# Normed residual steps of an eight-stage transformer kernel, in token halves: the end of each down product, the norm's sum from rounded parts, and the first three up blocks

## The reference, cut to what matters

```python
def rms_norm(x, g):
    xf = x.astype(jnp.float32)
    y = xf * lax.rsqrt(jnp.mean(xf * xf, axis=-1, keepdims=True) + EPS)
    return (y * g.astype(jnp.float32)).astype(x.dtype)

# first block, for each of 2 layers
hn = rms_norm(x, norm_mix_pre[layer])
m = mixer(hn, ...)                      # ends in ... @ w_out
x = x + rms_norm(m, norm_mix_post[layer])
hn = rms_norm(x, norm_ffn_pre[layer])
f = conv_geglu_ffn(hn, ...)             # ends in ... @ w_down
x = x + rms_norm(f, norm_ffn_post[layer])
```

## Time and profile before

| | |
|---|---|
| median of three executions | 2587.75 us |
| the profiled execution, first to last instruction | 2586.1 us |
| TensorE busy | 2557.9 us, 99% |
| VectorE busy | 1661.4 us, 64% |
| ScalarE busy | 1273.8 us, 49% |
| GpSimd busy | 360.5 us, 14% |
| granted TensorE clock, mean | 0.999 of full |

### The profile page before, as it was taken

One profiled execution on the slowest core, in us unless ns is written; L12 is line 12 of the kernel. 1 busy time (PEld: TensorE's weight loads), 2 busy tenths in 40 slices (PEclk: granted clock), 3 DMA queues, 4 the chain that ended last, 5 costly groups with the idle time before them and its releaser, 6 DMA issues.

```text
span 2586.1 us, 35264 instructions
## 1 busy us (share of the span) xinstructions
PE 2557.9 (99%) x12636; PEld 2031.6 (79%) x12636; DVE 1661.4 (64%) x2384; ACT 1273.8 (49%) x2129; POOL 360.5 (14%) x270
## 2 busy tenths in 40 slices
PE   9999999999999999999999999999999999999999
PEld 7855788888787557788888775789988777899887
DVE  4476677643988895677653777587633546687533
ACT  4326544333546895444333577567533425567432
POOL 0020100000103781100000130000610002000800
PEclk9999999999999999999999999999999999999999
DMA  5330222222233442222222230132232221232222
GB/s 215 107 93 25 96 98 97 97 98 95 82 135 118 135 131 73 85 98 94 97 98 97 95 103 1 60 120 99 88 107 96 92 104 50 98 123 99 82 97 97
DMA packets 74689, 250.44 MB, mean 97 GB/s; under 512 B 8748, under 2 KB 8876, under 8 KB 74192
## 3 DMA queue, kind: packets, MB, share of 16 engines
q1 hardware_dynamic: 73488, 240.63, 27.1%
q0 software_dynamic: 944, 8.33, 0.9%
q10 hardware_dynamic: 144, 0.00, 0.0%
HBM read 242.50 MB, written 2.24 MB: 95 GB/s over the span
## 4 chain that ended last, share of the span: by engine, by line
PE 90%; DVE 4%; ACT 2%; issue 1%; POOL 1%; SPq 0%; DMA 0%; DVEq 0%; ACTq 0%; POOLq 0%
PE bank L409 25%; PE bank L410 24%; PE bank L411 24%; PE bank L2199 2%; PE bank L1302 2%; PE bank L1304 2%; PE bank L1303 2%; POOL xT L852 1%; DVE mT L477 1%; PE bank L2751 1%; PE bank L3097 1%; PE bank L1647 1%; PE bank L1636 1%; PE bank L2206 1%; ACT arena L2826 0%
## 5 line engine op out<-in xcount | busy, mean ns | idle before, releaser
L383 DVE TENSOR_TENSOR wlo<-wraw,whi 128x1024 fp32r<-128x1024 f32 x349 | 447.7, 1284 | 444.6 <-ACT whi L360 444.0
L360 ACT ACTIVATE whi<-wraw 128x1024 fp32r<-128x1024 f32 x357 | 375.9, 1055 | 497.6 <-DMA wraw<-in_w 497.5
L409 PE MATMUL bank<-hnhi,whi 128*128 128x512 f32 (+1 forms) x1528 | 596.3, 390 | 0.8 <-DVE wlo L383 0.5
L410 PE MATMUL bank<-hnlo,whi 128*128 128x512 f32 (+1 forms) x1528 | 584.5, 382 | 0.0
L411 PE MATMUL bank<-hnhi,wlo 128*128 128x512 f32 x1392 | 542.1, 389 | 0.0
L409 PE MATMUL bank<-ahi,whi 128*128 128x512 f32 x1184 | 463.5, 391 | 1.8 <-DVE stats L2860 0.6
L410 PE MATMUL bank<-alo,whi 128*128 128x512 f32 x1184 | 460.8, 389 | 0.0
L411 PE MATMUL bank<-ahi,wlo 128*128 128x512 f32 x1184 | 460.8, 389 | 0.0
L409 PEld LDWEIGHTS bank<-hnhi,whi 128*128 128x128 f32 x1528 | 287.3, 188 | 85.1 <-issue 29.2
L410 PEld LDWEIGHTS bank<-hnlo,whi 128*128 128x128 f32 x1528 | 287.4, 188 | 57.8 <-issue 3.4
L411 PEld LDWEIGHTS bank<-hnhi,wlo 128*128 128x128 f32 x1392 | 261.3, 188 | 55.2
(11 more groups left out here) (356 smaller groups left out, 3918.8 us busy)
## 6 DMA issues: line engine op xcount, KB each, us to landing
wraw<-in_w SPq DMA_DIRECT2D x410, 512.0 KB, 3.3
arena<-cs_scratch SPq DMA_DIRECT2D x20, 512.0 KB, 6.0
over_a<-cs_scratch SPq DMA_DIRECT2D x12, 512.0 KB, 6.6
arena<-in_rpb POOLq DMA_DIRECT2D x1, 2880.0 KB, 14.0
out_dram<-xT SPq DMA_DIRECT2D x8, 256.0 KB, 2.0
arena<-in_t_step POOLq DMA_DIRECT2D x2, 897.0 KB, 4.7
mT<-arena SPq DMA_DIRECT2D x28, 64.0 KB, 2.0
arena<-in_t_ab POOLq DMA_DIRECT2D x1, 1472.0 KB, 6.6
```

The costliest lines, as they stand in the source:

```text
L360: act.activation(whi[:, slot * BLOCK:(slot + 1) * BLOCK], wraw[:, slot * BLOCK:(slot + 1) * BLOCK], ACT.Copy).then_inc(sem("w_hi"), 1)
L383: dve.tensor_tensor(low_home(i), wraw[:, slot * BLOCK:(slot + 1) * BLOCK], whi[:, slot * BLOCK:(slot + 1) * BLOCK], ALU.subtract).then_inc ...
L409: pe.matmul(out, wh, ah, start=start, stop=False)
L410: pe.matmul(out, wh, al, start=False, stop=False)
```

## The change

For `d` of 0 to 3, everything from the last two down tiles to the third up block is done in two halves of 256 tokens, A (tokens 0 to 255) and B.

- TensorE multiplies tile K-2 in full into banks 0 to 3 and for A alone into banks 4 to 7, then tile K-1 for A into all banks, then tile K-2 for B into banks 4 to 7, then tile K-1 for B.
- The squares of a half are all added by VectorE (seven additions for each half), the sum is split into a high part (ScalarE) and a low part (VectorE), and TensorE sums over the partitions in two fp32r matmuls of 256 columns, with ones rounded to fp32r, in place of three float32 ones. The five matmuls of `pe_busy` are gone.
- Rows of A are worked through (unit, x, high, low), then rows of B. VectorE updates x for rows 0, 1 and 4 of each half, GpSimd for the other five.
- Up blocks 0 to 2 take A for all eight rows, then B, with block 2 four rows behind.
- The next norm's partition sum stands at row 4 of block 3, before it was at row 1.

The core of the diff:

```diff
+        def pe_up_halves(pe, b0, norm):
...
+            for i, c in enumerate(HALVES):
+                for s in range(KT + LAG):
+                    if s < KT:
+                        pe.wait_ge(sem("norm_hi"), ROWS_BEFORE[norm] + 8 * i + s + 1)
...
+                    k = s - 1
+                    if 0 <= k < KT:
+                        pe.wait_ge(sem("hn_ready"), ROWS_BEFORE[norm] + 8 * i + k + 1)
...
+                    k = s - LAG
+                    if k >= 0:
...
+                        if i == 0 and k == SUM_AT_ROW:
+                            pe_post_sum(pe, d, 1)
...
+        def pe_down_halves(pe, name, K, d):
...
+            ready(K - 2)
+            for m in range(KT):
+                if m < 4:
+                    pe_product(pe, name, At(K - 2), m)
+                else:
+                    half(K - 2, m, 0)
+            ready(K - 1)
+            for m in range(KT):
+                half(K - 1, m, 0, True).then_inc(sem("down_done"), 1)
+            for m in range(4, KT):
+                pe.wait_ge(sem("post_sq"), squared(d, 0, m))
+                mm = half(K - 2, m, HALF)
+            mm.then_inc(sem("w_used"), 1)
+            for m in range(KT):
+                if m == 0:
+                    pe.wait_ge(sem("post_added"), added(d, "scaled"))
+                if m == 3:
+                    pe_post_sum(pe, d, 0)
+                half(K - 1, m, HALF, True).then_inc(sem("down_done" if m < KT - 1 else "w_used"), 1)
...
-            for m in range(KT):
-                wait_down(act, name, K, d, m)
-                act.activation(post_sq(m), bank[m][:, :], ACT.Square).then_inc(sem("post_sq"), 1)
-            act_split(act, At(FIRST[name] + K + 2))
...
+            act_split(act, At(nxt + 1))
+            act.activation(round_ones(), ones, ACT.Copy)
             for m in range(KT):
...
+                square(0, m)
+            square(1, 0)
+            raw(0)
+            sum_high(0)
+            square(1, 1)
+            raw(1)
+            square(1, 2)
+            raw(2)
+            root(0)
+            for m in range(3, KT):
+                square(1, m)
+                if m == 5:
+                    high(0, 0)
+                if m == 6:
+                    high(0, 1)
+            act_split(act, At(nxt + 2))
+            for m in range(2, KT):
+                high(0, m)
+            sum_high(1)
+            root(1)
+            for m in range(KT):
+                high(1, m)
+                act_square(act, m)
...
+            def rows(i, lag, after):
+                for m in range(KT + lag):
+                    if m < KT:
+                        unit(i, m)
+                        if m in X_BY_DVE:
+                            x_add(i, m)
+                    if m >= lag:
+                        low(i, m - lag)
+                    after(m)
+
+            def between(m):
+                if m == 3:
+                    dve_split(dve, At(FIRST[name] + K + 2))
+                if m >= 7:
+                    add(1, m - 4)
+
+            dve_split(dve, At(FIRST[name] + K + 1))
+            dve.wait_ge(sem("post_sq"), squared(d, 0, 0))
+            dve.tensor_scalar(mt(0)[:, 0:HALF], bank[0][:, 0:HALF], col(g, g0), None, ALU.mult).then_inc(sem("post_added"), 1)
+            for m in range(1, KT):
+                add(0, m)
+            sum_low(0)
+            add(1, 1)
+            add(1, 2)
+            rows(0, 2, between)
+            add(1, 6)
+            add(1, 7)
+            sum_low(1)
+            rows(1, 2, lambda m: None)
```

More of the change, by code:

```diff
@@ L576, in pe_up @@
                         mm = three(pe, bank[m.base % 4][:, :], w_parts(i, k * P), hn_parts(k), k == 0, k == KT - 1)
-                        if m.r is None and m.base == first and k == (1 if norm in POSTED else 3):
+                        if m.r is None and m.base == first and k == (4 if norm in POSTED else 3):
                             pe_norm_sum(pe, norm)
@@ L721, in pe_down @@
                     mm.then_inc(sem("w_used"), 1)
-            skew = K - 1 - last
-            for s in range(KT + 2 * skew):
-                if s in (0, 2 * skew):
+            if d < 4:
+                pe_down_halves(pe, name, K, d)
+                return
+            for s in range(KT + 2):
+                if s in (0, 2):
                     k = last + (s > 0)
@@ L727, in pe_down @@
                     pe.wait_ge(sem("w_lo"), b0 + k + 1 + extra(b0))
-                if skew and s < KT:
+                if s < KT:
                     mm = part(At(K - 2), s)
@@ L806, in pe_busy @@
[L806 to L819 removed]
+        SUM_BANKS = (0, 3)
@@ new lines, in wait_half, with squared @@
+        def wait_half(eng, name, K, d, i, m):
+            if i and m == KT - 1:
+                eng.wait_ge(sem("w_used"), FIRST[name] + K + extra(FIRST[name]))
+            else:
+                eng.wait_ge(sem("down_done"), 15 * d + 8 * i + m + 1)
+        SQUARES = ([(0, m) for m in range(KT)] + [(1, 0), ("raw", 0), (0, "sum"), (1, 1), ("raw", 1), (1, 2), ("raw", 2)]
+                   + [(1, m) for m in range(3, KT)] + [(1, "sum")])
+        def squared(d, i, m):
+            return len(SQUARES) * d + SQUARES.index((i, m)) + 1
@@ new lines, in build, with added, post_gain, square @@
+        ADDED = {"scaled": 1, ("sum", 0): 2, ("low", 0): 3, ("sum", 1): 4, ("low", 1): 5}
+        def added(d, what):
+            return len(ADDED) * d + ADDED[what]
+        def post_gain(d, m):
+            return POST[d][0], POST[d][1] + m
+        def act_post(act, name, K, d):
+            g, g0 = NORM_G[d + 1]
+            nxt = FIRST[name] + K
+            def square(i, m):
+                c = HALVES[i]
+                wait_half(act, name, K, d, i, m)
+                act.activation(post_sq(m, c), bank[m][:, c:c + HALF], ACT.Square).then_inc(sem("post_sq"), 1)
+            def raw(m):
+                act.activation(mt(m)[:, HALF:SEQ], bank[m][:, HALF:SEQ], ACT.Copy, scale=col(*post_gain(d, m)))\
+                    .then_inc(sem("post_sq"), 1)
+            def sum_high(i):
+                act.wait_ge(sem("post_added"), added(d, ("sum", i)))
+                act.activation(post_parts(HALVES[i])[0], post_sq(0, HALVES[i]), ACT.Copy).then_inc(sem("post_sq"), 1)
+            def root(i):
+                act.wait_ge(sem("post_sum"), 2 * d + i + 1)
+                act_rsqrt(act, post_sum(i), rstd[:, HALVES[i]:HALVES[i] + HALF], 1.0 / DM, EPS, "post_rstd")
+            def high(i, m):
+                c = HALVES[i]
+                act.wait_ge(*x_added(d, i, m))
+                act.activation(hn_parts(m)[0][:, c:c + HALF], xt(m)[:, c:c + HALF], ACT.Copy, scale=col(g, g0 + m))\
+                    .then_inc(sem("norm_hi"), 1)
+            act_split(act, At(nxt + 1))
+            act.activation(round_ones(), ones, ACT.Copy)
+            for m in range(KT):
+                square(0, m)
[21 more added lines that the diff above has]
+                act_square(act, m)
@@ new lines, in pe_post_sum @@
+        def pe_post_sum(pe, d, i):
+            pe.wait_ge(sem("post_added"), added(d, ("low", i)))
+            if i:
+                pe.wait_ge(sem("post_unit"), 16 * d + SUM_BANKS[1] + 1)
+            else:
+                pe.wait_ge(sem("post_sq"), squared(d, "raw", 0))
+            high, low = post_parts(HALVES[i])
+            pe.matmul(post_sum(i), round_ones(), high, start=True, stop=False)
+            pe.matmul(post_sum(i), round_ones(), low, start=False, stop=True).then_inc(sem("post_sum"), 1)
@@ L848, in pool_post, with sum_low @@
-        def pool_post(pool, d):
-            pool.wait_ge(sem("x_ready"), 8 * d + 3)
-            for m in range(3, KT):
-                pool.wait_ge(sem("post_unit"), 10 * d + m + 3)
-                pool.tensor_tensor(xt(m), xt(m), mt(m), ALU.add).then_inc(sem("x_ready"), 1)
+            def sum_low(i):
+                high, low = post_parts(HALVES[i])
+                dve.wait_ge(sem("post_sq"), squared(d, i, "sum"))
+                dve.tensor_tensor(low, post_sq(0, HALVES[i]), high, ALU.subtract).then_inc(sem("post_added"), 1)
@@ new lines, in unit @@
+            def unit(i, m):
+                c = HALVES[i]
+                y, by = mt(m)[:, c:c + HALF], rstd[:, c:c + HALF]
+                if m == 0:
+                    dve.wait_ge(sem("post_rstd"), 2 * d + i + 1)
+                if i == 0:
+                    dve.wait_ge(sem("post_sq"), squared(d, "raw" if m < 3 else 1, m))
+                if m == 0 and i == 0:
+                    dve.wait_ge(sem("post_added"), added(d, "scaled"))
+                if m == 0 or i and m < 3:
+                    dve.tensor_tensor(y, y, by, ALU.mult).then_inc(sem("post_unit"), 1)
+                else:
+                    dve.scalar_tensor_tensor(out=y, in0=bank[m][:, c:c + HALF], scalar=col(g, g0 + m), in1=by,
+                                             op0=ALU.mult, op1=ALU.mult).then_inc(sem("post_unit"), 1)
@@ L854, in dve_add, with pool_post @@
+        def pool_post(pool, d):
```

(6 more changed lines are left out.)

167 lines of the change are left out of this document (86 added, 81 removed).

## The result

The changed kernel takes 2612.51 us (median of 4 runs, 2612.41 to 2615.72) where the kernel before takes 2587.89 beside it (4 runs, 2585.64 to 2588.18): ratio 1.0101, 95% interval 1.0089 to 1.0112. The forecast was 2614, slower, with 2601 to 2626 as its range. The profiled execution took 2612.59 us, its span is 2610.8, 24.7 us longer than the 2586.1 of before.

A forecast was written before the change was run, and what follows sets the result against it. The prediction took VectorE and GpSimd, not TensorE, to set the pace near the four normed residuals. +6.5 us a transition, four times, gave +26 on 2586.1, so 2612.1, and with the median's 1.65, 2614 us; range 2601 to 2626.

The forecast's parts named there:

- The sum: One transition, start of tile K-2 to block 4: 47.8 us against 41.3, so +6.5, four times, +26.
- Root of A: First half's root, counted from tile K-2's start: +12.45 us, 1.2 earlier than before, with a TensorE stall of 1.2.
- Rows of A: VectorE's stretch on half A after its root: 11.6 us of work, with waits 13.6, to +26.1.
- Root of B: Second half's root, starting only after A's rows: VectorE idle for 1.5 us, resuming at +27.6.
- Rows of B: VectorE's work on half B: units and x 4.4 us, lows 3.3, waits 1.4, together 9.1, to +36.7.
- ScalarE keeps up: In half B's rows, ScalarE at 0.4 + 0.6 us a row was to keep up beside VectorE.
- Stretch and tail: VectorE from first root to last low part: 24.2 us against 16.4; then norm sum at +42.9, block 4 at +47.8.
- Rival 2: TensorE gets the lower clock in the transitions: +9 us a transition, 2650 if all four; chance 2%.
- Rival 1: Each of ten GpSimd additions of 0.70 us stops VectorE entirely: +4.1 us a transition, 2630; chance 5%.
- Rival 3: The change wins: with VectorE's stretch under 17.4 us TensorE is the bound, 2.3 us a transition gained, 2579; chance 5%.

The follow-up runs named there:

- e8: Changed kernel plus three unused float32 matmuls of 256 columns, only in TensorE's gap before B's first up row: 2612.86 us.
- e1: Changed kernel plus unused float32 matmuls in three TensorE waits (4 behind A's root, 5 before B's partition sum, 6 before B's first up row): 2615.63 us.
- e9: Changed kernel with the norm sum of block 3 back at its second row in place of its fifth: 2610.44 us.
- e6: Kernel before, with VectorE's unit rows 2 to 7 and all low parts as two instructions of 256 columns: 2603.73 us, ratio 1.0066.
- e11: Kernel before, with only unit rows 2 to 7 as two instructions of 256 columns, low parts whole: 2587.53 us against 2586.74, ratio 1.0002.
- e12: Kernel before, with x's last row added by VectorE and only rows 3 to 6 by GpSimd: 2585.01 us against 2587.19, ratio 0.9991.
- e4: Changed kernel with B's five additions of squares, high and low sum and partition sum moved up among A's rows: 2615.52 us.
- e7: Changed kernel with B's last five additions and low sum in one piece behind the split of block K+2, high sum, root and partition sum moved accordingly: 2611.68 us.
- e10: e7 with B's sum right behind A's fourth row, four idle matmuls ahead of it, and B's root one row earlier on ScalarE: 2606.28 us.
- e3: Changed kernel plus 16 matmuls of 256 columns on zeros in A's up rows of every transition, and one more ScalarE copy: 2613.2 us.
- e5: Changed kernel, but VectorE adds all eight rows of x in each half and GpSimd none: 2619.31 us.

## Why the prediction was right

**The sum.** +6.5 a transition was predicted, +5.85, +6.70, +5.77 and +6.65 came: 26 against 24.97. The walk over VectorE's queue, tail included, was right in its mechanism and 3 us too long: without the clock's part the transitions come 5.69, 5.79, 5.68 and 5.81 us above before (e8), 23.0 in all. The clock, at nothing in the sum, added 2.0. That the total came within 1 us is luck to that extent.

**Root of A.** +12.45 predicted, +12.27 measured; the stall at TensorE's sum 0.89, not 1.2.

**Rows of A.** 13.6 predicted, 13.2 measured (283.27 to 296.46, when the low sum lets go). The allowance for GpSimd was made of the wrong pieces. In a row of alternating unit and low part it is under 0.1 and not 0.15; the 0.5 for one addition that meets GpSimd head on was right (0.96 for 0.42), and the split paid 0.32 that was not in the sum.

**Root of B.** 1.5 of idle time predicted, 1.55 in the row. B's first unit at +27.6 predicted, +27.1 measured.

**Rows of B.** 9.1 predicted, 8.85 measured, though for another reason at the end: there ScalarE, with 0.92 us for a high part and a square of a row, is the slower engine, and VectorE waits 0.33 and 0.37 for it. "ScalarE keeps up" was wrong by that.

**Stretch and tail.** 24.2 predicted, 23.7 measured. Block 4 at +47.8 predicted, 47.14 and 47.04 measured in the first and third transition, where the tail ran as walked: the wait before block 4 is 1.66 against 1.9.

**The step that failed** is the one on the clock. Rival 2 got 2%, because a window of before with 0.8 us of idle time had kept clock 1.00 and the longest gap would be 1.7 us. In the change it fell in all four transitions. The trace of before could have warned: it has a fall behind gaps of 1.26 and 1.84 us at 1558. The price was also not what the rival said: not 9 us a transition but about 0.9, in the second and fourth, since most of TensorE's slow time lay beside VectorE's stretch (e1, e8). There the fall began 27.9 and 27.7 us after the first half matmul, in the first and third 26.1 and 25.9, so TensorE had less time to catch up before the norm sum. The norm sum's later place, which the prediction put at a gain of 0.1, made this loss possible (e9).

**Rival 1** was argued away by the wrong view of the row. "GpSimd stops VectorE entirely" is what e6, e11 and e12 show for VectorE's instructions with two inputs from SBUF; what the prediction took as evidence against it, 1.04 in place of 0.66 for a low part, is by these runs the remainder of GpSimd's addition after `unit` from PSUM has covered the rest. The number in the sum was right because the change also alternates unit and low part; e4 and e6 show how wrong it becomes where the order does not give that cover. The price of 2630 for the rival counted every addition in full and so missed this cover.

**Rival 3** needed B's root under A. e4 put it there and lost; e7 and e10 show that it can be had for 6.2 us of the 25, if the additions stay clear of GpSimd and TensorE is kept from most of the lower clock. The rest is, as far as the prediction's walk tells, what it said: two halves on VectorE for one whole, and B's rows behind A's.

**What stays open.** How e10's 19.5 us divide between the halves' fixed cost and B's rows behind A's was not measured apart. What exactly makes the clock fall was not looked for. The gap of 1.41 us had a fall behind it in all four transitions of the change; with more work ahead of the same gap (e3) it had one in the second and fourth, and there the norm sum was late again (40.0 and 40.2 us after the first half matmul). The gap of 2.53 us before block 4 had a fall behind it in e4, e5, e7 and e8 and none in the change, e1, e3 or e10.

## What to carry to other kernels

Cutting a tile in halves to start a consumer sooner pays only if the engine that produces the halves has room for the doubled number of instructions, and for the second half's share standing behind the first; count that engine's queue before anything else. Where VectorE and GpSimd both work from SBUF, plan them as one resource, one whole instruction of either at a time, and put VectorE's work from PSUM under GpSimd's instruction: halving the low parts cost 16 us here, halving `unit` 0.8, within the noise. A gap of TensorE can cost more than itself where the work behind it runs at half clock, as behind the 1.41 us here; see whether something that is waited for stands in that work, and leave it be if not. And a chain of waits that runs over a busy engine does not prove that this engine sets the pace: here it named TensorE, and giving TensorE its full clock moved VectorE's last low part by nothing.

## What the runs showed of the hardware that was not expected

- The granted clock fell to the lower level behind gaps of only 1.41 us (299.58), with 2.23 us of work in the 4.5 before its end, and 1.78 us (e8, 1494.35), with matmuls close behind each other before it. In e7 it fell behind gaps of 0.88, 0.85 and 0.63 in a row (287.4). Of several gaps of like length in one kernel some had a fall behind them and some not, and keeping one gap busy (e8) went with falls at two others.
- GpSimd's addition of x is shown with 1.39 to 1.47 us where it had waited for `unit` (e6), and with a median of 1.74 where five follow each other: the difference is, by the order seen in e6, its own wait for VectorE's low part; it was not measured apart. Its 256-column form shows 0.70 alone and 0.91 beside VectorE.
- A VectorE instruction with two inputs from SBUF that meets such an addition is held to about its end, whatever its own length: 256 columns were held for 0.54 (0.96 less 0.42) by a half addition and for up to 1.03 (1.51 less 0.48) by a whole one.
